# The end of a mixture-of-experts block: the last two experts' results scattered together, the last 2 MB of weights loaded by columns

## The chip, the cores and the metric

One core of a Trainium2 chip runs the kernel. The metric is the device time of one execution in microseconds (us); of several executions the median is given.

## The reference

One residual block on x of 256 tokens x 1024, in float32. The first part is sparse attention and a pooling mixer, merged and added to x. The second part, which takes four fifths of the time, is a mixture of 32 experts of which each token takes 4:

```
logits = tok @ router_w + router_b
topv, topi = top_k(logits, 4);  topw = softmax(topv)
combine = sum(one_hot(topi, 32) * topw[..., None], axis=1)
for e in range(32):
    gu = tok @ w1[e] + b1[e]                       # 1024 -> 2048
    gate = minimum(gu[:, :1024], 7);  lin = clip(gu[:, 1024:], -7, 7)
    act = (lin + 1) * gate * sigmoid(1.702 * gate)
    out = out + combine[:, e:e + 1] * (act @ w2[e] + b2[e])
x = x + out
```

`w1[e]` is 8 MB and `w2[e]` 4 MB.

## The kernel before, in words

Every expert gets 64 slots. For expert e the kernel gathers the rows of its tokens by a matmul with a 0/1 matrix (`pick`, L362), multiplies them with `w1` (`up`, L399), applies the gate on DVE and ACT, transposes the activation, multiplies with `w2` (`down`, L428), and adds the result to the tokens' rows by a matmul with a matrix that holds each slot's token and weight (`scatter`, L437). A loop with five experts in each turn does that with one expert's `up` ahead of the `down` of the one before.

The weights come from HBM in chunks of 2 MB, in pairs where that is possible, into a ring of ten slots; the DMAs stand in one queue, issued by SP, which waits until a slot's reader is done. Every chunk of `w2` holds 4 of the 8 rows that each partition has of it. Of the last chunks SP loads pieces with semaphores of their own: the table `TAIL` (L185) gives the rows of each. `(E - 2, 1)` and `(E - 1, 0)` are halves of 1 MB, and `(E - 1, 1)`, the last 2 MB, comes in parts of 1, 0.5 and 0.5 MB (`load_tail`, L598 to L602).

Everything of 64 slots uses half of the PE array. In `down` an expert's 64 x 1024 result is cut in two halves of 512 columns. The left one goes to partitions 0 to 63 of a bank of PSUM and the right one to partitions 64 to 127 of the same bank, so each matmul has 64 columns of the array and two of them stand one behind the other on its two column halves. One ACT copy brings the bank to SBUF (`out_out`, L846). In `scatter` the 64 slots are the rows of the array, again in pairs: the left result sits on partitions 0 to 63, the right one on 64 to 127, and the placement matrix, transposed, is there twice (`putT`, 128 partitions). For each of the two token tiles (`tt`) and each half it adds to one of four accumulator banks: bank `2 * tt + half`. These four hold the sum over all experts for the whole run.

The order of PE's work is written out by hand. At the end, behind the loop (from the call of `up_last`), it is:

```
down_tail(E - 1, 0, ps_gather, actT_last)
pe.wait_ge(out_ok, E - 1)
scatter(pe, None, range(0, 1))
down_tail(E - 1, 1, ps_gather, actT_last).then_inc(gemm2, 1)
scatter(pe, None, range(1, 2))
pe.wait_ge(out_ok, E)
scatter(pe, acc_done, range(TT), putT_last, out_last)
```

The first two scatters are those of expert 30, whose result ACT copies at L846; the last one is expert 31's, copied at L877, with its placement copied at L871. Then two of the four result tiles are finished by DVE (L1200, with an addition of x) and stored by SP (L635), the other two are copied by ACT (L895), and after both copies ACT issues their stores (L899). SP waits for all four stores.

Of the kernel before, what the change touches and what calls it, by code (L numbers as in the profile page):

```python
# [24 lines left out]
P = 128  # L25
# [15 lines left out]
def block_kernel(nc, x, attn_norm_g, w_in, q_norm_g, k_norm_g, pool_w, pool_b, pool_scale,  # L41
# [44 lines left out]
    with ExitStack() as ctx:  # L86
        def sb(name, shape, dt=F32):
            return ctx.enter_context(nc.sbuf_tensor(name, shape, dt))
# [40 lines left out]
        putT_last, actT_last, out_last = work[:, 5, 0:TT * P], work[:, 6], work[:, 7]  # L129
# [4 lines left out]
        putT = sb("putT", [P, TT * P])  # L134
        bias_pick = sb("bias_pick", [P, SLOTS])
# [39 lines left out]
        ps_gate, ps_lin, ps_out, ps_gather = bank[4:8]  # L175
        first_ps = (ps_gather, bank[3])
# [7 lines left out]
        HALVES, THIRDS = ((0, 2), (2, 4)), ((0, 2), (2, 3), (3, 4))  # L184
        TAIL = {(E - 2, 1): HALVES, (E - 1, 0): HALVES, (E - 1, 1): THIRDS}  # L185
# [3 lines left out]
        def tail_in(e, c, i):  # L189

            return part_in[tail_parts.index((e, c, i))]
# [150 lines left out]
        def w2_wide(e):  # L342

            return expert_w2[0][bass.ds(e, 1), :, :].rearrange("a (p k) n -> p (a k n)", p=P)
# [87 lines left out]
        def scatter(pe, done=None, tiles=range(TT), at=putT, src=out_e):  # L432

            for tt in tiles:
                for half in range(2):
                    rows = halves(half)
                    mm = pe.matmul(acc[2 * tt + half][:, :], at[rows, tt * P:(tt + 1) * P], src[rows, :],  # L437
                                   start=False, stop=True, skip_group_check=True)
                    if done is not None:
                        mm.then_inc(done, 1)  # L440
            return mm
# [30 lines left out]
        def _(sp):  # L472
# [125 lines left out]
            def load_tail(e, c):  # L598

                src = w2_wide(e)[:, c * CHUNK_N:(c + 1) * CHUNK_N]  # L600
                for i, (a, b) in enumerate(TAIL[e, c]):
                    sp.dma_start(chunk_slot(w2_chunk(e, c))[:, a * D:b * D], src[:, a * D:b * D]).then_inc(tail_in(e, c, i), 16)  # L602
# [77 lines left out]
        def _(act):  # L680
# [190 lines left out]
            nc.scalar.copy(putT_last, ps_gather[:, 0:T]).then_inc(put_sb, 1)  # L871
# [3 lines left out]
            out_out(E - 2)  # L875
            act.wait_ge(gemm2, E)
            nc.scalar.copy(out_last, ps_gather[:, :]).then_inc(out_ok, 1)  # L877
# [15 lines left out]
            for tt, j in enumerate((1, 2)):  # L893
                act.wait_ge(acc_done, j + 1)
                nc.scalar.copy(xs[:, tt, (1 - tt) * BANK:(2 - tt) * BANK], acc[j][:, :]).then_inc(s["result_act"], 1)  # L895
            for tt in range(TT):
                cols = slice((1 - tt) * BANK, (2 - tt) * BANK)
                act.wait_ge(s["result_act"], tt + 1)
                act.dma_start(out[0, tt * P:(tt + 1) * P, cols], xs[:, tt, cols]).then_inc(s["stored"], 16)  # L899
# [304 lines left out]
        def _(pe):  # L1204
# [374 lines left out]
            def down_tail(e, c, ps, actT):  # L1579
                for i, (a, b) in enumerate(TAIL[e, c]):  # L1580
                    pe.wait_ge(tail_in(e, c, i), 16)
                    mm = down(pe, chunk_halves(w2_chunk(e, c)), c, range(a, b), ps, actT, True)
                return mm

# [58 lines left out]
            down_tail(E - 1, 0, ps_gather, actT_last)  # L1643
            pe.wait_ge(out_ok, E - 1)
            scatter(pe, None, range(0, 1))
            down_tail(E - 1, 1, ps_gather, actT_last).then_inc(gemm2, 1)
            scatter(pe, None, range(1, 2))
            pe.wait_ge(out_ok, E)
            scatter(pe, acc_done, range(TT), putT_last, out_last)
# [53 lines left out]
```

## Time and profile before

| what | us |
|---|---|
| median of 3 runs | 1113.23 (1112.6 to 1114.18) |
| the profiled execution, its own time | 1112.02 |
| its span, from the first to the last instruction | 1110.3 |
| PE busy | 1075.9 (97%) |
| DMA of the weights, 430.73 MB in the SP queue | 92.1% of 16 engines' span |
| DVE busy, ACT busy | 216.3, 160.8 |

The time of a run holds some 1.7 us that lie outside of the span. PE's busy time is that of overlapping matmuls, which are modelled to their ends, so 97% does not say that PE sets the pace: it waits for the weights in nearly every expert. The chain that ended last names DMA for 33% of the span and PE for 64%.

### The profile page before, as it was taken

The numbers are of one execution on the slowest core, as the hardware profiler recorded it, in microseconds if no ns is written. First come the engines' busy times: TensorE is split into PE (matmuls) and PEld (weight loads), VectorE is DVE, ScalarE is ACT, GpSimd is POOL, SyncE is SP. The second block draws the span as 40 slices with busy tenths as digits, with TensorE's granted clock in tenths as the row PEclk, the third lists the DMA queues.
The fourth block names the chain that finished last, engine by engine and source line by source line (L and its number), as shares of the span: only waits on it lengthen the run. The fifth ranks groups of instructions, "written<-read, shape, count | busy, mean of one in ns | idle before, by whom it ended". The sixth has DMA issues, their size and how long they took to land.

```text
span 1110.3 us, 12071 instructions
## 1 busy us (share of the span) xinstructions
PE 1075.9 (97%) x5114; PEld 458.5 (41%) x5114; DVE 216.3 (19%) x521; ACT 160.8 (14%) x362; POOL 20.5 (2%) x38
## 2 busy tenths in 40 slices
PE   9999999999999999999999999999999999999997
PEld 6478885633333333333333333333233333333332
DVE  2722121321111111211111111111111111111111
ACT  2114201210000111111111111111011111111111
POOL 0006000000000000000000000000000000000000
PEclk9999999999999999999999999999999999999999
DMA  9924627999999999999999999999999999999996
GB/s 338 378 80 150 226 87 319 400 421 429 426 423 424 432 429 433 427 437 430 432 430 431 433 433 433 430 430 430 433 433 433 431 430 430 431 434 432 426 427 276
DMA packets 34891, 432.60 MB, mean 390 GB/s; under 512 B 3612, under 2 KB 5168, under 8 KB 17712
## 3 DMA queue, kind: packets, MB, share of 16 engines
q1 hardware_dynamic: 32672, 430.73, 92.1%
q10 hardware_dynamic: 2192, 1.48, 0.5%
q8 instruction: 21, 0.34, 0.1%
q14 instruction: 6, 0.05, 0.0%
HBM read 431.15 MB, written 1.05 MB: 389 GB/s over the span
## 4 chain that ended last, share of the span: by engine, by line
PE 64%; DMA 33%; DVE 2%; issue 0%; ACT 0%; SPq 0%
DMA ring<-in_expert_w_dram 32%; PE bank L399 24%; PE bank L428 14%; PE bank L1330 5%; PE bank L437 4%; PE bank L1394 2%; PE bank L362 2%; PE bank L1404 2%; PE bank L389 2%; PE bank L1253 2%; PE bank L1314 1%; PE bank L376 1%; PE bank L411 1%; PE bank L381 1%; PE bank L1226 1%; DVE ring L967 1%
## 5 line engine op out<-in xcount | busy, mean ns | idle before, releaser
L399 PE MATMUL bank<-ring,work 128*64 128x512 f32 x2048 | 451.5, 596 | 15.6 <-DMA ring<-in_expert_w_dram 15.6
L399 PEld LDWEIGHTS bank<-ring,work 128*64 128x64 f32 x2048 | 143.3, 137 | 320.8 <-issue 289.6
L428 PE MATMUL bank<-ring,work 128*64 128x512 f32 x992 | 219.4, 593 | 11.4 <-DMA ring<-in_expert_w_dram 11.3
L428 PEld LDWEIGHTS bank<-ring,work 128*64 128x64 f32 x992 | 74.9, 137 | 151.2 <-issue 148.9
L1104 DVE TENSOR_SCALAR work<-bank 128x512 f32<-128x512 f32 x31 | 21.4, 692 | 459.8 <-PE bank L399 459.8
L826 ACT ACTIVATE work<-work 128x512 f32<-128x512 f32 x31 | 19.5, 630 | 497.7 <-DVE work L1104 497.7
L463 DVE TENSOR_TENSOR work<-bank,vecs 128x512 f32<-128x512 f32 x31 | 21.4, 691 | 209.9 <-PE bank L376 209.9
L437 PE MATMUL bank<-work,putT 64*128 64x512 f32 x248 | 61.9, 616 | 0.0
L362 PE MATMUL bank<-xs,pick 128*64 128x512 f32 x248 | 58.5, 592 | 0.0
L1330 PE MATMUL bank<-ring 128*128 128x256 f32 x256 | 56.6, 380 | 0.0
L1330 PEld LDWEIGHTS bank<-ring 128*128 128x128 f32 x256 | 48.2, 190 | 6.7 <-issue 0.3
L846 ACT COPY work<-bank 128x512 f32<-128x512 f32 x31 | 18.2, 587 | 203.4 <-PE bank L428 203.4
L1253 PE MATMUL bank<-ring 128*128 128x512 f32 x96 | 42.3, 595 | 0.0
L418 ACT COPY work<-bank 64x256 f32<-64x256 f32 (+1 forms) x112 | 40.2, 359 | 3.7 <-PE bank L411 2.7
L389 PE MATMUL bank<-b_rows,bias_pick 32*64 32x512 f32 x256 | 34.8, 612 | 0.3 <-ACT work L837 0.3
L362 PEld LDWEIGHTS bank<-xs,pick 128*64 128x64 f32 x248 | 17.7, 137 | 35.0 <-issue 35.0
L437 PEld LDWEIGHTS bank<-work,putT 64*128 64x128 f32 x248 | 21.3, 186 | 19.4 <-issue 15.8
L1404 PE MATMUL bank<-ring,xn 128*128 128x512 f32 (+1 forms) x80 | 28.4, 508 | 0.0
L1114 DVE TENSOR_TENSOR work<-work 128x512 f32<-128x512 f32 x26 | 27.5, 1057 | 0.9
L1253 PEld LDWEIGHTS bank<-ring 128*128 128x128 f32 x96 | 17.9, 190 | 21.0 <-issue 20.9
L454 DVE TENSOR_SCALAR put<-slot_id,place,weight 128x128 f32<-128x128 f32 x64 | 19.3, 343 | 37.6 <-PE bank L381 37.5
L1108 DVE SCALAR_TENSOR_TENSOR work<-work 128x512 f32<-128x512 f32 x31 | 21.4, 692 | 3.2
(210 smaller groups left out, 523.7 us busy)
## 6 DMA issues: line engine op xcount, KB each, us to landing
ring<-in_expert_w_dram SPq DMA_DIRECT2D x70, 4096.0 KB, 39.5
ring<-in_expert_w_dram SPq DMA_DIRECT2D x39, 2048.0 KB, 15.9
ring<-in_expert_w_dram SPq DMA_DIRECT2D x21, 1024.0 KB, 10.5
ring<-in_w_in_dram SPq DMA_DIRECT2D x8, 2048.0 KB, 21.0
ring<-in_w_out_dram SPq DMA_DIRECT2D x2, 2048.0 KB, 8.1
ring<-in_w_branch_attn_dram SPq DMA_DIRECT2D x1, 2048.0 KB, 7.9
ring<-in_w_branch_pool_dram SPq DMA_DIRECT2D x1, 2048.0 KB, 8.9
work<-in_expert_w_dram SPq DMA_DIRECT2D x2, 1024.0 KB, 13.7
```

The lines of the kernel that those rows point to most:

```text
L362: mm = pe.matmul(ps_gather[SLOTS * half:SLOTS * (half + 1), :], pick[:, tt, :], xs[:, tt, half * BANK:(half + 1) * BANK], start=(tt == 0), ...
L389: mm = pe.matmul(dst, bias_pick[rows, :], b1_rows[rows, :], start=first, stop=not first, skip_group_check=True)
L399: mm = pe.matmul(dst, hTe[:, at:at + SLOTS], w[a][:, col:col + BANK], start=(k == 0 and not bias_first), stop=(k == KD - 1 and bias_first) ...
L418: last = nc.scalar.copy(dst[halves(h), :].rearrange("p (j i s) -> p i j s", i=2, s=SLOTS)[:, i, blocks, :], src[halves(i), :].rearrange("p ...
L428: mm = pe.matmul(ps[SLOTS * half:SLOTS * (half + 1), :], actT[:, at:at + SLOTS], w[a // 2][:, col:col + BANK], start=(k == 0), stop=(k == ...
L437: mm = pe.matmul(acc[2 * tt + half][:, :], at[rows, tt * P:(tt + 1) * P], src[rows, :], start=False, stop=True, skip_group_check=True)
L463: return nc.vector.tensor_tensor(hTe.rearrange("p (j h n) -> p j h n", j=4, h=2), ps_gather[:, :].rearrange("p (j h n) -> p j h n", j=4, h ...
L1114: nc.vector.tensor_tensor(by_rows(act_e), lin, sig, ALU.mult).then_inc(glu_ok, 1)
L1253: mm = pe.matmul(dst, hT[:, k, tt * P:(tt + 1) * P], w[:, k, :], start=(k == 0), stop=(k == KD - 1))
L1330: mm = pe.matmul(bank[GATE_BANK[n % 4]][:, b * T:(b + 1) * T], w[:, k, at:at + P], hT[:, k, :], start=(k == 0), stop=(k == KD - 1))
L1394: mm = pe.matmul(bank[2 + 2 * (j % 2) + n][:, b * T:(b + 1) * T], w[:, k, at:at + P], src[:, k, :], start=(k == 0), stop=(k == KA - 1))
L1404: mm = pe.matmul(ps, mergedT[:, k, tt * P:(tt + 1) * P], w[:, k, at:at + cols.stop - cols.start], start=(k == 0), stop=(k == KD - 1))
```

## The change

The last 2 MB of `w2` are cut by columns: first the left 512 columns of all four rows (1 MB), then the right 512 columns of two rows and of the other two (0.5 MB each). For expert 31 the halves of the result go to two banks, the left one to partitions 64 to 127 of bank 7 and the right one to partitions 0 to 63 of bank 5. ACT copies expert 30's left half to partitions 0 to 63 of a tile and expert 31's left half to partitions 64 to 127 of the same tile, and so, the other way round, for the right halves; the placements are put together likewise. One scatter matmul with 128 rows then adds both experts' results to an accumulator bank: first the left half for both token tiles, then the right half. ACT stores each of its tiles right behind its copy. Expert 31's chunk 1 no longer has a scatter ahead of it.

```diff
-        putT_last, actT_last, out_last = work[:, 5, 0:TT * P], work[:, 6], work[:, 7]
+        actT_last = work[:, 6]
+        two_out = (xn[:, 0, 0:BANK], xn[:, 0, BANK:D])
...
+        two_putT = (putT, xn[:, 1, 0:TT * P])
...
+        last_ps = (ps_gather, ps_lin)
...
-        HALVES, THIRDS = ((0, 2), (2, 4)), ((0, 2), (2, 3), (3, 4))
-        TAIL = {(E - 2, 1): HALVES, (E - 1, 0): HALVES, (E - 1, 1): THIRDS}
+        HALVES, COLUMNS = ((0, 2, 0, D), (2, 4, 0, D)), ((0, 4, 0, BANK), (0, 2, BANK, D), (2, 4, BANK, D))
+        TAIL = {(E - 2, 1): HALVES, (E - 1, 0): HALVES, (E - 1, 1): COLUMNS}
...
-                src = w2_wide(e)[:, c * CHUNK_N:(c + 1) * CHUNK_N]
-                for i, (a, b) in enumerate(TAIL[e, c]):
-                    sp.dma_start(chunk_slot(w2_chunk(e, c))[:, a * D:b * D], src[:, a * D:b * D]).then_inc(tail_in(e, c, i), 16)
+                src = w2_wide(e)[:, c * CHUNK_N:(c + 1) * CHUNK_N].rearrange("p (r n) -> p r n", n=D)
+                dst = chunk_slot(w2_chunk(e, c)).rearrange("p (r n) -> p r n", n=D)
+                for i, (a, b, left, right) in enumerate(TAIL[e, c]):
+                    sp.dma_start(dst[:, a:b, left:right], src[:, a:b, left:right]).then_inc(tail_in(e, c, i), 16)
...
             act.wait_ge(put_ps, E)
-            nc.scalar.copy(putT_last, ps_gather[:, 0:T]).then_inc(put_sb, 1)
+            act.wait_ge(put_sb, E - 1)
+            chain.link(nc.scalar.copy(two_putT[1][halves(1), :], putT[halves(1), :]))
+            nc.scalar.copy(two_putT[1][halves(0), :], ps_gather[halves(0), 0:T])
+            nc.scalar.copy(two_putT[0][halves(1), :], ps_gather[halves(1), 0:T]).then_inc(put_sb, 1)
...
-            out_out(E - 2)
-            act.wait_ge(gemm2, E)
-            nc.scalar.copy(out_last, ps_gather[:, :]).then_inc(out_ok, 1)
+            act.wait_ge(gemm2, E - 1)
+            nc.scalar.copy(two_out[0][halves(0), :], ps_out[halves(0), :])
+            nc.scalar.copy(two_out[1][halves(1), :], ps_out[halves(1), :]).then_inc(out_ok, 1)
+            for h in range(2):
+                act.wait_ge(gemm2, E + h)
+                nc.scalar.copy(two_out[h][halves(1 - h), :], last_ps[h][halves(1 - h), :]).then_inc(out_ok, 1)
...
-            for tt, j in enumerate((1, 2)):
-                act.wait_ge(acc_done, j + 1)
-                nc.scalar.copy(xs[:, tt, (1 - tt) * BANK:(2 - tt) * BANK], acc[j][:, :]).then_inc(s["result_act"], 1)
-            for tt in range(TT):
+            for n, tt in enumerate((1, 0)):
                 cols = slice((1 - tt) * BANK, (2 - tt) * BANK)
-                act.wait_ge(s["result_act"], tt + 1)
+                act.wait_ge(acc_done, n + 2)
+                nc.scalar.copy(xs[:, tt, cols], acc[1 + tt][:, :]).then_inc(s["result_act"], 1)
+                act.wait_ge(s["result_act"], n + 1)
                 act.dma_start(out[0, tt * P:(tt + 1) * P, cols], xs[:, tt, cols]).then_inc(s["stored"], 16)
...
+            def down_last(c, i):
+
+                a, b, left, right = TAIL[E - 1, c][i]
+                w = chunk_halves(w2_chunk(E - 1, c))
+                pe.wait_ge(tail_in(E - 1, c, i), 16)
+                for r in range(a, b):
+                    k = c * W2_ROWS + r
+                    for half in range(left // BANK, right // BANK):
+                        col = r % 2 * D + half * BANK
+                        mm = pe.matmul(last_ps[half][halves(1 - half), :], actT_last[:, k * SLOTS:(k + 1) * SLOTS],
+                                       w[r // 2][:, col:col + BANK], start=(k == 0), stop=(k == KD - 1))
+                return mm
+
+            def scatter_two(half):
+
+                for tt in range(TT):
+                    pe.matmul(acc[2 * tt + half][:, :], two_putT[half][:, tt * P:(tt + 1) * P], two_out[half],
+                              start=False, stop=True, skip_group_check=True).then_inc(acc_done, 1)
...
-            down_tail(E - 1, 0, ps_gather, actT_last)
-            pe.wait_ge(out_ok, E - 1)
-            scatter(pe, None, range(0, 1))
-            down_tail(E - 1, 1, ps_gather, actT_last).then_inc(gemm2, 1)
-            scatter(pe, None, range(1, 2))
-            pe.wait_ge(out_ok, E)
-            scatter(pe, acc_done, range(TT), putT_last, out_last)
+            for i in range(2):
+                down_last(0, i)
+            down_last(1, 0).then_inc(gemm2, 1)
+            down_last(1, 1)
+            down_last(1, 2).then_inc(gemm2, 1)
+            for half in range(2):
+                pe.wait_ge(out_ok, E + half)
+                scatter_two(half)
```

PE's order from the last expert's chunk 1 on. Before (of its eight scatter matmuls the last two, on banks 2 and 3, follow behind the rows; `part_in4` to `part_in6` are the three parts of the last 2 MB, banks 0 to 3 the accumulators):

```order
L437 MATMUL bank0<-work,putT 128x512 [waits out_ok]
L437 MATMUL bank1<-work,putT 128x512
L428 MATMUL bank7<-ring,work 64x512 [waits part_in4]
L428 MATMUL bank7<-ring,work 64x512 x3
L428 MATMUL bank7<-ring,work 64x512 [waits part_in5]
L428 MATMUL bank7<-ring,work 64x512
L428 MATMUL bank7<-ring,work 64x512 [waits part_in6]
L428 MATMUL bank7<-ring,work 64x512
L437 MATMUL bank2<-work,putT 128x512
L437 MATMUL bank3<-work,putT 128x512
L437 MATMUL bank0<-work 128x512 [waits out_ok]
L437 MATMUL bank1<-work 128x512
```

The same place with the change:

```order
L1603 MATMUL bank7<-ring,work 64x512 [waits part_in4]
L1603 MATMUL bank7<-ring,work 64x512 x3
L1603 MATMUL bank5<-ring,work 64x512 [waits part_in5]
L1603 MATMUL bank5<-ring,work 64x512
L1603 MATMUL bank5<-ring,work 64x512 [waits part_in6]
L1603 MATMUL bank5<-ring,work 64x512
L1610 MATMUL bank0<-xn,putT 128x512 [waits out_ok]
L1610 MATMUL bank2<-xn,putT 128x512
L1610 MATMUL bank1<-xn 128x512 [waits out_ok]
L1610 MATMUL bank3<-xn 128x512
```

Four scatter matmuls have gone, among them the two that stood ahead of the first part; the four left matmuls of the chunk now stand together ahead of the four right ones.

ACT's order from expert 31's gate to the last copy of a result, before:

```order
L869 ACTIVATE work<-work 128x64x4 [waits gate_ok] x2
L871 COPY work<-bank 128x256 [waits put_ps]
L418 COPY work<-bank 64x2x64 [waits actT_ps]
L418 COPY work<-bank 64x2x64 x3
L418 COPY work<-bank 64x2x64 [waits actT_ps]
L418 COPY work<-bank 64x2x64 x3
L846 COPY work<-bank 128x512 [waits glu_ok,gemm2]
L877 COPY work<-bank 128x512 [waits gemm2]
```

And with the change:

```order
L873 ACTIVATE work<-work 128x64x4 [waits gate_ok] x2
L876 COPY xn<-putT 64x256 [waits put_sb,put_ps]
L877 COPY xn<-bank7 64x256 [waits act_step]
L878 COPY putT<-bank7 64x256
L421 COPY work<-bank4 64x2x64 [waits actT_ps]
L421 COPY work<-bank4 64x2x64 x3
L421 COPY work<-bank5 64x2x64 [waits actT_ps]
L421 COPY work<-bank5 64x2x64 x3
L883 COPY xn<-bank6 64x512 [waits gemm2]
L884 COPY xn<-bank6 64x512
L887 COPY xn<-bank7 64x512 [waits gemm2]
L887 COPY xn<-bank5 64x512 [waits gemm2]
```

One copy of the placement has become three, and two copies of results four, each of 64 partitions.

## Rows read from the trace of the kernel before

**Rows 1.** Chain that ended last, in order of time from 1055 us: start, us, what
```profile
core 0 of [0], span 1110.3 us
...
1055.85 39.88 DMA ring<-in_expert_w_dram
...
1098.76 3.58 PE bank L428 x16
1102.35 2.83 PE bank L437 x12
...
1105.19 0.69 DVE xs L1200
```
**Rows 2.** Timeline of PE, 1095 to 1105 us: start, us, engine, line, operation, shapes, records
```profile
1095.76 0.20 PEld L428 LDWEIGHTS bank<-ring,work 128*64 128x64 f32 x4 [1.19 <-DMA ring<-in_expert_w_dram]
1095.77 1.94 PE L428 MATMUL bank<-ring,work 128*64 128x512 f32 x8 [0.30 <-DMA ring<-in_expert_w_dram]
1097.63 1.13 PE L437 MATMUL bank<-work,putT 64*128 64x512 f32 x4
1098.69 3.65 PE L428 MATMUL bank<-ring,work 128*64 128x512 f32 x16
...
1101.75 0.60 PE L428 MATMUL bank<-ring,work 128*64 128x512 f32 x2
1102.28 1.13 PE L437 MATMUL bank<-work,putT 64*128 64x512 f32 x4
1103.24 1.88 PE L437 MATMUL bank<-work 64*128 64x512 f32 x8
```
**Rows 3.** Timeline of PE, 11 to 26 us: matmuls that are not in pairs
```profile
11.17 1.89 PE L1231 MATMUL bank<-ring 128*68 128x256 f32 x8
...
18.53 7.03 PE L1253 MATMUL bank<-ring 128*128 128x512 f32 x16
```
**Rows 4.** Stretches: 2 KB rows alone, then the experts' loads; last columns PEclk, DMA share, GB/s
```profile
40.00:45.00 5.00, 5.00 (x13) 2.24 (x12) 4.42 (x17) 0.60 (x1) 0.00 (x0) 1.00 1.05 387
1060.00:1070.00 10.00, 10.00 (x50) 3.79 (x46) 2.47 (x4) 2.67 (x7) 0.00 (x0) 1.00 1.00 428
```
**Rows 5.** Timeline of ACT, 1086 to 1103 us
```profile
1086.97 0.36 ACT L871 COPY work<-bank 128x256 f32<-128x256 f32 x1
1089.98 2.18 ACT L418 COPY work<-bank 64x128 f32<-64x128 f32 x8 [2.65 <-PE bank L411]
1093.79 0.59 ACT L846 COPY work<-bank 128x512 f32<-128x512 f32 x1 [1.64 <-PE bank L428]
1102.39 0.59 ACT L877 COPY work<-bank 128x512 f32<-128x512 f32 x1 [8.02 <-PE bank L428]
```
**Rows 6.** Stores by SP (L635), by ACT (L899); DMA from 1104 to 1111 us in 40 slices
```profile
1105.01 0.35 SPq L635 DMA_DIRECT2D out_dram<-xs  x1
1105.91 1.20 SPq L635 DMA_DIRECT2D out_dram<-xs  x1
DMA to landing us min/median/max: 2.5/3.3/4.0
DMA to landing us min/median/max: 3.6/3.6/3.7
GB/s 0 0 0 0 0 0 0 0 94 0 117 351 374 398 363 351 374 363 176 23 117 386 398 398 398 386 374 386 199 23 23 12 0 0 0 0 0 0 0 0
```
**Rows 7.** PE after long waits (timeline), and stretches around them with PEclk
```profile
672.55 0.65 PE L399 MATMUL bank<-ring,work 128*64 128x512 f32 x2 [0.86 <-DMA ring<-in_expert_w_dram]
789.18 8.78 PE L399 MATMUL bank<-ring,work 128*64 128x512 f32 x32 [2.16 <-DMA ring<-in_expert_w_dram]
934.95 2.37 PE L399 MATMUL bank<-ring,work 128*64 128x512 f32 x10 [2.15 <-DMA ring<-in_expert_w_dram]
...
790.00:792.00 2.00, 2.00 (x8) 0.51 (x6) 0.00 (x0) 0.00 (x0) 0.00 (x0) 0.50 0.91 393
792.00:794.00 2.00, 2.00 (x10) 0.66 (x8) 0.00 (x0) 0.00 (x0) 0.00 (x0) 0.67 1.03 442
934.00:936.00 2.00, 1.05 (x6) 0.48 (x8) 0.00 (x0) 0.00 (x0) 0.00 (x0) 1.00 1.06 459
```

More of the change, by code:

```diff
@@ L430, in down, with scatter @@
             return mm
-        def scatter(pe, done=None, tiles=range(TT), at=putT, src=out_e):
-            for tt in tiles:
+        def scatter(pe, done=None):
+            for tt in range(TT):
                 for half in range(2):
                     rows = halves(half)
-                    mm = pe.matmul(acc[2 * tt + half][:, :], at[rows, tt * P:(tt + 1) * P], src[rows, :],
+                    mm = pe.matmul(acc[2 * tt + half][:, :], putT[rows, tt * P:(tt + 1) * P], out_e[rows, :],
                                    start=False, stop=True, skip_group_check=True)
@@ L1579, in down_tail @@
             def down_tail(e, c, ps, actT):
-                for i, (a, b) in enumerate(TAIL[e, c]):
+                for i, (a, b, left, right) in enumerate(TAIL[e, c]):
                     pe.wait_ge(tail_in(e, c, i), 16)
@@ L1583, in down_tail @@
                 return mm
+            def down_last(c, i):
[10 more added lines that the diff above has]
+            def scatter_two(half):
+                for tt in range(TT):
+                    pe.matmul(acc[2 * tt + half][:, :], two_putT[half][:, tt * P:(tt + 1) * P], two_out[half],
+                              start=False, stop=True, skip_group_check=True).then_inc(acc_done, 1)
             def gather_expert(e):
```

## The prediction

> **What bounds the kernel now.** I read the chain of waits first. For the last 55 us it has one DMA entry, which ends at 1095.73 (1055.85 + 39.88), and after it nothing but PE, one DVE addition and what follows it [rows 1]. So up to 1095.7 the stream of weights sets the time. The change leaves that stretch as it is, and everything is decided in the 14.6 us behind it. The timeline of PE shows them: the second half of expert 31's chunk 0 (8 records, from 1095.77), the first two scatter matmuls of expert 30 (4 records, 1097.63), chunk 1 (16 records, 1098.69), the other two of expert 30 (1102.28), and expert 31's four (8 records, 1103.24) [rows 2]. Each fp32 matmul of the program leaves two records. Then come an addition of 0.69 us, from 1105.19 [rows 1], the last store, issued at 1105.91 and landed 4.0 us later, at 1109.9 [rows 6], and 0.4 us to the end of the span.
>
> The unit of PE's time: 16 records of two column halves take 3.65 us [rows 2]. Two start together every 0.429 us (7 x 0.429 + 0.64 = 3.64), so a pair of program matmuls on the two halves costs 0.858 us, and the halves run side by side. Records that have the array to themselves are no cheaper: 16 of 512 elements take 7.03 us (15 x 0.429 + 0.59), and eight with only 68 active columns and 256 elements take 1.89 us, 0.216 each [rows 3].
>
> **The change, part by part.** All sums run against the profiled execution: span 1110.3, its own time 1112.02, which is 1.2 below the median of the three runs, 1113.23.
>
> (a) The last 2 MB come in rows of 2 KB (512 columns) instead of 8 and 4 KB. In the stretch where this kernel loads 2 KB rows alone the DMA moves 387 GB/s; near the end it moves 428 [rows 4]. Left half: 1.049 MB / 387 = 2.71 us, landing at 1095.73 + 2.71 = 1098.44; now the same bytes need 2.45, 1098.18. The two right quarters follow at 1099.79 and 1101.15. The bounds of this term are 0 (428) and +0.26 us on the left half. I take +0.26, since the rows of that size are the nearest. The three parts were handed over long before they move, so their issue hides behind the 40 us of queue [rows 1].
>
> (b) Expert 30's first two scatter matmuls leave the gap in which PE waits for chunk 1. They cost nothing there but about 0.25 us (PE starts chunk 1 at 1098.69, though the bytes are due at 1098.18). After the change PE starts the left half at 1098.44 + 0.04 = 1098.48, 0.2 earlier than now, and idles about 0.9 us before it.
>
> (c) Chunk 1 loses its pairs. Its left half is four matmuls on one column half of the array (bank 7), its right half four on the other (bank 5). By rows 3 four unpaired matmuls take 4 x 0.858 = 3.43 us, as long as all eight take now. Left ones start at 1098.48, 1099.34, 1100.20 and 1101.05. The first right matmul stands directly behind the last left one, on the other half. Such neighbours start together now: four weight loads within 0.20 us, and 8 records in 1.94 us = 3 x 0.429 + 0.65 [rows 2], with the second half's first pass not held up by the first half's second pass. So I let them overlap by one matmul: the right four run from 1101.05 to 1104.48, both quarters landed before they are due (1101.05 and 1102.77). Now the same work ends at 1101.75 + 0.43 = 1102.18. The term is **+2.3 us**. From below: the halves run freely from their landings, 1099.8 at the earliest (-1.2 us). From above: no overlap (+0.86).
>
> (d) The scatter now comes whole behind it. Before: 6 program matmuls in three pairs, from 1102.28. After: 4 with all 128 rows, which fill the array and can't pair. Their first record starts 0.52 us after the last one of the right half, as at the switch of 1101.75 to 1102.28 [rows 2]: 1104.05 + 0.52 = 1104.57. Eight records by 0.429: the last starts at 1104.57 + 3.00 = 1107.57, against 1104.53 now (1103.24 + 1.88 - 0.59). With (c) that makes **+3.0 us** on PE; the scatter's own share is 0.75.
>
> (e) ACT. The left copy is released 0.64 us after the last left record starts (1101.48; as 1101.75 to 1102.39 now [rows 2, 5]), takes 0.59 and is done at 1102.7, well before 1104.57. The right one: 1104.05 + 0.64 + 0.59 = 1105.28, needed by the third scatter matmul at 1106.29, so it is hidden with 1.0 us left; without that cover the 0.5 us wait of today's copy would come back. Copying 64 partitions instead of 128 I count at the full 0.59. Expert 30's copy becomes two, 1.18 us from 1093.8, and nobody asks for them before 1104. The placement's copy (0.36 at 1086.97) becomes three and a wait, 1.2 us, into an idle stretch that lasts until 1089.98 [rows 5]. All zero.
>
> (f) The stores. Results now leave PE 0.86 us apart instead of two and two, so the last addition starts at 1107.57 + 0.66 = 1108.23, ends at 1108.92 and its store is issued at 1108.95. Today the last of four stores, all issued within 0.9 us, lands after 4.0 us, and the first of its queue after 2.5 [rows 6]. The first bytes move 0.85 us after the first issue, and 256 KB at some 370 GB/s take 0.7 [rows 6]. Bounds for the new last store: 1.9 us (0.85, 0.7 and the 0.35 that the end of the span shows behind the last landing) and 4.0. I take 2.2, between 1.9 and the 2.5 of the store that had its engines nearly alone: **-1.8 us**. The Trainium skill ("DMA: Bandwidth & Descriptors", section on latency) gives a DMA a fixed cost of about 2 us, most of it the receipt from memory; with 0.6 for the bytes that would be 2.6, and the sum 0.4 higher. No row shows a store alone.
>
> Sum: 1108.95 + 2.2 + 0.4 = 1111.5, against 1110.3: +3.0 - 1.8 = **+1.2 us**. On the median: 1113.2 + 1.2 = **1114.4 us**. That is 0.1%, inside the 0.2% (2.2 us) that a measurement of this kernel can tell from no change.
>
> **The rivals.**
>
> A, the forecast: one matmul of overlap between the halves, short last store; 0.44, 1114.4.
>
> B, no such overlap: the right half's first pass waits for the last left matmul's second pass, at 1101.48, or for its end, 1101.91. The 1.94 us for 8 records [rows 2] speak against it, since strict order of passes would give 1.72 + 0.59 = 2.31. Price +0.43 to +0.86, 1114.8 to 1115.3; 0.15. The Trainium skill ("TensorE: Matmul & The Clock Gate", Part 3, the mechanism of packing small matmuls) has this rule: matmuls start and end strictly in program order.
>
> C, the halves run apart. PE looks further ahead, and the right half starts with its landings: 1099.83, 1100.69, 1101.55, 1102.41, end 1103.26. The scatter's last record starts at 1106.35 and all ends 1.2 earlier: 1113.2. For it: pairs already pass each other by a pass. Against: nothing shows a longer lead. 0.18.
>
> D, a lone column half streams at twice the rate. The left half would end at 1100.2, the right one with its last quarter at 1102.1, the scatter's last record start at 1105.4: 2.2 less, 1112.2. The 68-column rows [rows 3] speak against it. 0.05; only together with a very short store is this faster by over 0.2%.
>
> E, the slower side: the store saves nothing. Behind each pair of stores the DMA moves 23 GB/s for a while, one engine's worth [rows 6]; if that engine is late for another reason than four stores at once, the last store takes 4.0 us as now, and the whole delay of PE shows: +3.0, 1116.2. It decides from a landing of 3.2 us upward (+2.2). For it: the ACT queue's first store took 3.6 us, with hardly more beside it than its fellow's 2.5 [rows 6]. 0.13.
>
> F, the clock. The removed scatter makes PE idle for about 0.9 us. After an idle of 2.16 us the granted clock was 0.50 from 790 to 792, 1.2 GHz instead of 2.4, and 0.67 over the next 2 us, which costs 2 x 0.50 + 2 x 0.33 = 1.7 us; an equal idle at 932 to 935 and one of 0.86 at 672 changed nothing [rows 7]. Price +1.7: 1116.1. 0.05.
>
> **How the numbers follow.** A to D lie between 1112.2 and 1115.3, E and F at 1116. The range 1112.4 to 1116.0 takes in A, B and C with their bounds and some of E. Faster by over 0.2% (under 1111.0) needs D and more: 0.05. Slower by over 0.2% (over 1115.4) is E, F and the upper edge of B with a store of 2.6: 0.20. The rest, 0.75, is no change.
>
> **What would show each step.** (a) PE's first record of the left half near 1098.5, DMA near 390 GB/s in the last 5 us. (b) An idle of about 0.9 us on PE before it, named DMA, clock at 1.0. (c) The lone left records 0.429 us apart, the first right record with the seventh left one; all 16 in 6.0 us (6.9 in B, 4.8 in C). (d) Eight scatter records in 3.6 us with no gap between the third and the fourth, and 0.52 us before the first. (e) No wait on ACT's copy in front of the third scatter matmul. (f) Four stores issued about 0.9 us apart, the last landing 2.2 us after its issue; 2.6 or 4.0 would name the page's figure or E. The forecast is wrong if lone halves run at another pace than 0.429 us a record, or if the last store does not gain at least 1 us.

## The result, and the profile after

Over 21 runs each the change takes 1114.42 us (median; 1112.85 to 1115.92) and the kernel before 1113.21 us (1111.47 to 1114.46). The ratio is 1.0014 with an interval of 1.0008 to 1.002: a little slower, inside of the 0.2% that the prediction called no change. The medians lie 1.2 us apart. The profiled executions have spans of 1111.3 and 1110.3 us, so of that they show 1.0.

The chain that ended last, in order of time from 1060 us (start, us, what), answers to [rows 1]:

```profile
1059.97 38.35 DMA ring<-in_expert_w_dram
1098.32 0.04 issue
1098.37 5.42 PE bank L1603 x16
1103.79 3.65 PE bank L1610 x8
1107.43 0.02 issue
1107.45 0.69 DVE xs L1209
```

The weights' stream still ends the wait at which the tail begins, but one part later, at 1098.32. Behind it stand 5.42 us of chunk 1 where 3.65 stood, then the scatter, the addition and the store. The timeline of PE and of its weight loads (PEld) over the same stretch, with the idle time ahead in brackets, answers to [rows 2]:

```profile
1095.65 1.94 PE L1603 MATMUL bank<-ring,work 128*64 128x512 f32 x8 [0.35 <-DMA ring<-in_expert_w_dram]
1098.37 5.42 PE L1603 MATMUL bank<-ring,work 128*64 128x512 f32 x16 [0.77 <-DMA ring<-in_expert_w_dram]
...
1099.28 0.14 PEld L1603 LDWEIGHTS bank<-ring,work 128*64 128x64 f32 x1 [0.29 <-issue]
1099.70 0.14 PEld L1603 LDWEIGHTS bank<-ring,work 128*64 128x64 f32 x1 [0.29 <-issue]
1100.13 0.19 PEld L1603 LDWEIGHTS bank<-ring,work 128*64 128x64 f32 x3 [0.29 <-issue]
1100.56 0.19 PEld L1603 LDWEIGHTS bank<-ring,work 128*64 128x64 f32 x2 [0.24 <-issue]
...
1103.72 1.98 PE L1610 MATMUL bank<-xn,putT 128*128 128x512 f32 x4
...
1105.11 0.19 PEld L1610 LDWEIGHTS bank<-xn 128*128 128x128 f32 x1 [0.24 <-issue]
1105.54 1.88 PE L1610 MATMUL bank<-xn 128*128 128x512 f32 x4
```

Up to 1099.70 one weight load stands every 0.43 us: the left matmuls alone. At 1100.13 there are three within 0.19 us. Two of them are the right half's, which joins beside the fifth left record. Between the two groups of scatter records nothing is lost: the eight start from 1103.72 to 1106.83 (1105.54 + 1.88 - 0.59). ACT's timeline, to be held against [rows 5]:

```profile
1086.93 0.40 ACT L876 COPY xn<-putT 64x256 f32<-64x256 f32 x1
1087.37 0.37 ACT L877 COPY xn<-bank 64x256 f32<-64x256 f32 x1
1087.74 0.37 ACT L878 COPY putT<-bank 64x256 f32<-64x256 f32 x1
1089.82 2.17 ACT L421 COPY work<-bank 64x128 f32<-64x128 f32 x8 [1.71 <-PE bank L414]
1093.63 0.58 ACT L883 COPY xn<-bank 64x512 f32<-64x512 f32 x1 [1.64 <-PE bank L431]
...
1102.05 0.58 ACT L887 COPY xn<-bank 64x512 f32<-64x512 f32 x1 [7.25 <-PE bank L1603]
1103.82 0.58 ACT L887 COPY xn<-bank 64x512 f32<-64x512 f32 x1 [1.19 <-PE bank L1603]
```

The last copy ends at 1104.40. The third scatter matmul starts at 1105.54 and its weight load, which waits for that copy, at 1105.11, so 0.7 us are left. A copy of 64 partitions takes 0.58, as long as one of 128 took. Three views answer to [rows 6]. The last store in SP's timeline:

```profile
1108.17 0.35 SPq L639 DMA_DIRECT2D out_dram<-xs  x1
```

The landings of the two stores of SP and of the two of ACT, by their lines:

```profile
DMA to landing us min/median/max: 2.6/2.7/2.8
DMA to landing us min/median/max: 2.8/3.0/3.2
```

The DMA from 1104 to 1111.3 in 40 slices:

```profile
GB/s 0 0 0 0 0 0 0 0 0 0 0 0 0 281 370 348 337 180 337 370 370 213 11 22 112 348 382 393 382 404 382 393 135 22 22 22 0 0 0 0
```

The last store takes 2.8 us from its issue to its landing where it took 4.0. In the stretch of the last 2 MB's left half the DMA moves 384 GB/s at a granted clock of 1.00 (last three columns: PEclk, DMA share, GB/s):

```profile
1095.70:1098.30 2.60, 1.89 (x8) 0.44 (x8) 0.00 (x0) 0.00 (x0) 0.00 (x0) 1.00 1.04 384
```

### The profile page after: what moved, and what is told of

Same layout as the page of the kernel before. It is cut to its first block, busy times and chain, and to the rows that moved or that the text cites. A ratio compares the mean times of both kernels' runs of the same rounds, so it can differ in the third digit from the quotient of the medians.

```text
span 1111.3 us, 12059 instructions
## 1 busy us (share of the span) xinstructions
PE 1077.7 (97%) x5106; PEld 459.4 (41%) x5106; DVE 216.3 (19%) x521; ACT 162.8 (15%) x366; POOL 20.6 (2%) x38
## 4 chain that ended last, share of the span: by engine, by line
PE 64%; DMA 32%; DVE 2%; SPq 0%; issue 0%; ACT 0%; POOL 0%; POOLq 0%
DMA ring<-in_expert_w_dram 32%; PE bank L402 24%; PE bank L431 13%; PE bank L1339 5%; PE bank L440 3%; PE bank L1403 2%; PE bank L365 2%; PE bank L1413 2%; PE bank L392 2%; PE bank L1262 2%; PE bank L1323 1%; PE bank L379 1%; PE bank L414 1%; PE bank L384 1%; PE bank L1235 1%; DVE ring L976 1%
## 5 line engine op out<-in xcount | busy, mean ns | idle before, releaser
L402 PE MATMUL bank<-ring,work 128*64 128x512 f32 x2048 | 451.5, 596 | 15.4 <-DMA ring<-in_expert_w_dram 15.4
L431 PE MATMUL bank<-ring,work 128*64 128x512 f32 x960 | 212.1, 593 | 11.1 <-DMA ring<-in_expert_w_dram 11.0
L440 PE MATMUL bank<-work,putT 64*128 64x512 f32 x240 | 59.6, 615 | 0.0
## 6 DMA issues: line engine op xcount, KB each, us to landing
work<-in_expert_w_dram SPq DMA_DIRECT2D x2, 1024.0 KB, 13.9
```

Source lines behind the costliest of these rows:

```text
L402: mm = pe.matmul(dst, hTe[:, at:at + SLOTS], w[a][:, col:col + BANK], start=(k == 0 and not bias_first), stop=(k == KD - 1 and bias_first) ...
L431: mm = pe.matmul(ps[SLOTS * half:SLOTS * (half + 1), :], actT[:, at:at + SLOTS], w[a // 2][:, col:col + BANK], start=(k == 0), stop=(k == ...
L440: mm = pe.matmul(acc[2 * tt + half][:, :], putT[rows, tt * P:(tt + 1) * P], out_e[rows, :], start=False, stop=True, skip_group_check=True)
```

## The experiments

Two theories stood at the start. **The lone halves** (matmuls for one column half of the array with none for the other beside them): the change loses time because chunk 1's matmuls no longer run in pairs, and the rest costs nothing on balance. **The column cut is sound**, and the cost comes from elsewhere (the scatter of 128 rows, smaller DMA rows, the order of the stores). A second question was open for the stores: what the last one waits for.

From one profiled execution to the next the whole end shifts by up to 2.2 us, since the stream of weights ends earlier or later (this start lies between 1095.47 and 1097.68). Traces are therefore compared by **the tail**: the span less the start of the second part of expert 31's chunk 0 on PE. It is 1110.3 - 1095.77 = 14.5 us before and 1111.3 - 1095.65 = 15.7 with the change. Every tail is that of one trace. x3_right_first (1118.0 us), x4_two_stores (1114.65), x6_lone_pieces (1116.23), x7_store_behind (1113.78), x10_no_second_pass (1112.87) and x11_before_no_second_pass (1111.78) ran once each, so for them only the trace speaks.

### By rows again, in pairs (x1_rows)

```diff
-        HALVES, COLUMNS = ((0, 2, 0, D), (2, 4, 0, D)), ((0, 4, 0, BANK), (0, 2, BANK, D), (2, 4, BANK, D))
+        HALVES, THIRDS = ((0, 2, 0, D), (2, 4, 0, D)), ((0, 2, 0, D), (2, 3, 0, D), (3, 4, 0, D))
...
-            down_last(1, 0).then_inc(gemm2, 1)
-            down_last(1, 1)
-            down_last(1, 2).then_inc(gemm2, 1)
+            for i in range(3):
+                mm = down_last(1, i)
+            mm.then_inc(gemm2, 2)
```

> Undoes the column cut alone: the last 2 MB by rows (1, 0.5, 0.5 MB) and in pairs, the two experts' scatter and the order of the stores stay. If the lone column halves are what the change pays with, the 16 records of chunk 1 take 3.65 us instead of 5.42, from about 1098.2; the left copy ends at about 1102.5, the first of 8 scatter records starts at 1102.6 (1103.72 with the change), the last at 1105.6 (1106.82), and the span is 1.1 to 1.2 us shorter than the change's 1111.3, about 1110.1. If instead the cut is what makes this end work (left copy and scatter early), taking it away exposes both ACT copies and the span is 1111.3 or more.

Ratio to the kernel before 0.9999 (0.999 to 1.0008), 1113.07 us. Timeline of PE:

```profile
1097.57 1.94 PE L1603 MATMUL bank<-ring,work 128*64 128x512 f32 x8 [0.30 <-DMA ring<-in_expert_w_dram]
1100.03 3.65 PE L1603 MATMUL bank<-ring,work 128*64 128x512 f32 x16 [0.53 <-DMA ring<-in_expert_w_dram]
1104.36 1.98 PE L1610 MATMUL bank<-xn,putT 128*128 128x512 f32 x4 [0.68 <-ACT xn L887]
```

The tail is 14.6 us (1112.2 - 1097.57), 1.0 less than the change's. The span alone, 1112.2, would speak for the other case of the expectation; but this execution (1113.98 us) was the slowest of eleven with a median of 1113.07, and its tail began 1.9 us later than that of the change's trace. Chunk 1 is back at 3.65 us. Against that, the left copy now stands open: PE idles 0.68 us for it. Both things were expected, and the first is the larger. The merged scatter and the new order of the stores together neither cost nor gain anything against the kernel before that these runs could tell.

### The column cut alone (x2_lone_halves)

The kernel before, with `load_tail` and `TAIL` of the change and a `down` that takes the sides:

```diff
-        def down(pe, w, c, rows=range(W2_ROWS), ps=ps_out, actT=actT_e, wide=False):
+        def down(pe, w, c, rows=range(W2_ROWS), ps=ps_out, actT=actT_e, wide=False, sides=range(2)):
...
-                for half in range(2):
+                for half in sides:
...
```

> The kernel before with the column cut alone: same parts as the change, chunk 1 as four left and then four right matmuls, but expert 30's and expert 31's scatters apart and placed as before, all stores as before. If lone halves cost 0.43 us a record with the right half starting beside the third left matmul, chunk 1's records span 5.4 us instead of 3.65, the last scatter record starts 1.8 to 1.9 us later (1106.4) and the span is 1112.1, ratio 1.0016. If the cut costs only the 0.2 us of its smaller DMA rows, the span is 1110.5.

Ratio 1.0014 (1.0005 to 1.0023), 1114.59 us. Timeline of PE:

```profile
1095.47 1.94 PE L428 MATMUL bank<-ring,work 128*64 128x512 f32 x8 [0.31 <-DMA ring<-in_expert_w_dram]
1097.34 1.13 PE L437 MATMUL bank<-work,putT 64*128 64x512 f32 x4
1098.40 5.42 PE L428 MATMUL bank<-ring,work 128*64 128x512 f32 x16
```

5.42 us again, and a tail of 16.3 (1111.8 - 1095.47), 1.8 over the kernel before. So the cut by columns alone costs 1.8 us in the trace, and undoing it alone gives 1.0 back. The difference is near the 0.68 us for which x1_rows waits for the left copy: in the change that copy lies under the right half's matmuls. Chunk 1 starts 2.93 us behind the start of the tail here and 2.92 before, so behind the two scatters, which keep PE busy past the landing, the smaller DMA rows cost nothing. That answers the first question: the loss comes from the lone halves.

### How far PE looks ahead (x3_right_first, x6_lone_pieces)

In the change the right half joined earlier than forecast. Either it only waited for its data, or PE lets it pass a fixed lead. First the right quarters are loaded ahead of the left half:

```diff
-                for i, (a, b, left, right) in enumerate(TAIL[e, c]):
+                order = (1, 2, 0) if (e, c) == (E - 1, 1) else range(len(TAIL[e, c]))
+                for i in order:
+                    a, b, left, right = TAIL[e, c][i]
```

> The change with the right quarters loaded ahead of the left half, PE's order unchanged: when the first left matmul starts (about 1101.0) all of the right half lies in SBUF. If PE looks a fixed way ahead, the first right record again starts with the fifth left one, 1.75 us behind the first, and the 16 records span 5.42 us. If in the changed kernel the right half only waited for its data, it starts within 0.1 us of the first left record and the 16 span 3.65 us. If the halves overlap by one matmul, as forecast, it starts with the seventh, 2.6 us behind.

The timeline of the weight loads:

```profile
1101.51 0.29 PEld L1605 LDWEIGHTS bank<-ring,work 128*64 128x64 f32 x2 [4.16 <-DMA ring<-in_expert_w_dram]
1102.42 0.23 PEld L1605 LDWEIGHTS bank<-ring,work 128*64 128x64 f32 x1 [0.62 <-issue]
1103.28 0.23 PEld L1605 LDWEIGHTS bank<-ring,work 128*64 128x64 f32 x1 [0.62 <-issue]
1104.13 0.23 PEld L1605 LDWEIGHTS bank<-ring,work 128*64 128x64 f32 x1 [0.62 <-issue]
1104.70 0.19 PEld L1605 LDWEIGHTS bank<-ring,work 128*64 128x64 f32 x3 [0.34 <-issue]
```

The stretches around them (the column ahead of the last two is PEclk):

```profile
1101.50:1103.50 2.00, 1.99 (x3) 0.74 (x4) 0.00 (x0) 0.00 (x0) 0.00 (x0) 0.50 0.00 0
1105.50:1108.00 2.50, 2.50 (x10) 0.74 (x6) 0.00 (x0) 0.58 (x1) 0.00 (x0) 1.00 0.00 0
```

The right half's data had been there since before 1101.5, and still it joins with the fifth left record, as in the change. So it is a limit on how far PE runs ahead, and not the data. The time in microseconds came out differently from what was expected (6.84 us for the 16 records), because PE had idled 3.28 us and the clock was granted at 0.50, 1.2 GHz: a left record takes 0.86 us there. The tail is 20.0 us, 4.3 over the change's: 2.5 from the longer wait for the left half, 1.4 from the clock (6.84 against 5.42), 0.4 at the last store.

Then pieces of 256 columns, all on the column half that the change uses:

```diff
-                        col = r % 2 * D + half * BANK
-                        mm = pe.matmul(last_ps[half][halves(1 - half), :], actT_last[:, k * SLOTS:(k + 1) * SLOTS],
-                                       w[r // 2][:, col:col + BANK], start=(k == 0), stop=(k == KD - 1))
+                        for q in range(2):
+                            at, col = q * QUARTER, r % 2 * D + half * BANK + q * QUARTER
+                            mm = pe.matmul(last_ps[half][halves(1 - half), at:at + QUARTER], actT_last[:, k * SLOTS:(k + 1) * SLOTS],
+                                           w[r // 2][:, col:col + QUARTER], start=(k == 0 and q == 0), stop=(k == KD - 1),
+                                           skip_group_check=True)
```

> The same pieces of 256 columns, but both on the column half that the change uses, so chunk 1 is eight unpaired left matmuls and eight unpaired right ones of 0.43 us each. It tells what PE counts in looking ahead: if it is instructions (two matmuls with their weight loads), the first right record starts with the 13th left one, 2.6 us behind the first, and the records of chunk 1 span about 6.3 us; if it is time (1.75 us behind the first, as in the change), with the 9th, and they span 5.4 us.

```profile
1100.08 6.31 PE L1605 MATMUL bank<-ring,work 128*64 128x256 f32 x32 [0.63 <-DMA ring<-in_expert_w_dram]
```

Every record is half as long and the 32 take 6.31 us, as the count by matmuls gives it: 16 left records at 0.216, of which the last four run beside the right half. The weight loads agree: behind the first two they stand singly, 0.215 us apart, up to 1102.51, and at 1102.73, 2.65 us behind the first, there are three within 0.19 us. Lead by time would have given 5.4. In three kernels the right half joins as the last but one of the left matmuls starts (each is two records), whether such a matmul takes 0.86 us or 0.43, and also in x3_right_first, where at half the clock 3.2 us had passed since the first.

### Pieces of 256 columns, in pairs (x5_quarters, x5_again)

The same pieces go to both column halves, so that each of the left and the right half is done in pairs:

```diff
...
+                        for q in range(2):
+                            col = r % 2 * D + half * BANK + q * QUARTER
+                            mm = pe.matmul(last_ps[half][halves(q), 0:QUARTER], actT_last[:, k * SLOTS:(k + 1) * SLOTS],
+                                           w[r // 2][:, col:col + QUARTER], start=(k == 0), stop=(k == KD - 1))
...
-                nc.scalar.copy(two_out[h][halves(1 - h), :], last_ps[h][halves(1 - h), :]).then_inc(out_ok, 1)
+                for q in range(2):
+                    last = nc.scalar.copy(two_out[h][halves(1 - h), q * QUARTER:(q + 1) * QUARTER], last_ps[h][halves(q), 0:QUARTER])
+                last.then_inc(out_ok, 1)
```

> The change with every 512-column half of expert 31's down matmuls cut in two pieces of 256 columns that go to the two column halves of the array, so that the left half and the right half of chunk 1 are each done in pairs; two more ACT copies. If unpaired halves are what the change pays with, chunk 1's 32 records end 1.4 us earlier against its first one than in the change, the scatter starts at 1102.0 instead of 1103.7, its last record at about 1105.1 instead of 1106.8, and the time is 1.5 to 1.7 us under the change: ratio to the kernel before 0.9995, 1112.7. If pieces of 256 columns cost more than half of 512 (weight loads of 0.14 us for matmuls of 0.22), or the two extra copies show, little is left of that and the ratio stays at 1.001.

```profile
1097.12 1.95 PE L1607 MATMUL bank<-ring,work 128*64 128x256 f32 x16 [0.43 <-DMA ring<-in_expert_w_dram]
1099.75 3.67 PE L1607 MATMUL bank<-ring,work 128*64 128x256 f32 x32 [0.68 <-DMA ring<-in_expert_w_dram]
1103.35 1.98 PE L1614 MATMUL bank<-xn,putT 128*128 128x512 f32 x4
1105.17 1.88 PE L1614 MATMUL bank<-xn 128*128 128x512 f32 x4
```

3.67 us and no wait for the copy: the tail is 14.0 us (1111.1 - 1097.12), 1.7 under the change and 0.5 under the kernel before, to 0.1 us as expected. The ratio is 1.0001 (0.9992 to 1.001). A second time:

> The version in pieces of 256 columns a second time, unchanged, beside the one with five parts: its trace was 0.55 us shorter than that of the kernel before between the second part of chunk 0 and the end, while its ratio was 1.0001 with an interval of 0.9992 to 1.001. If the trace tells the truth the ratio of this run lies at 0.9995; if something outside of the tail costs it 0.5 us, it stays at 1.000.

Ratio 1.0 (0.9991 to 1.0009), tail 13.9. The 0.5 us by which both traces are under the kernel before would be 0.9995, which both intervals hold; the timed runs can neither show nor refute it. Against the change the intervals meet only at their edges (1.0008 to 1.002 against 0.9992 to 1.001 and 0.9991 to 1.0009), and the tail is 1.7 to 1.8 us shorter in both traces.

### Five parts (x9_five_parts)

```diff
-        HALVES, COLUMNS = ((0, 2, 0, D), (2, 4, 0, D)), ((0, 4, 0, BANK), (0, 2, BANK, D), (2, 4, BANK, D))
+        HALVES, COLUMNS = ((0, 2, 0, D), (2, 4, 0, D)), ((0, 2, 0, BANK), (2, 4, 0, BANK), (0, 2, BANK, D), (2, 3, BANK, D), (3, 4, BANK, D))
...
-            down_last(1, 0).then_inc(gemm2, 1)
-            down_last(1, 1)
-            down_last(1, 2).then_inc(gemm2, 1)
+            for i in range(5):
+                mm = down_last(1, i)
+                if i in (1, 4):
+                    mm.then_inc(gemm2, 1)
...
```

> The version in pieces of 256 columns, with the last 2 MB in five parts instead of three: left half in 0.5 and 0.5 MB, right half in 0.5, 0.25 and 0.25 MB (two semaphores of the start of the kernel are used a second time). PE then need not wait for the whole left half, and only one row's matmuls (0.43 us) follow the last landing. If PE's late start on the left half is what delays its end, the last record of chunk 1 starts 5.4 us behind the first of the second part of chunk 0 instead of 5.9, and the span less that start is 13.5 us instead of 14.0; ratio to the kernel before 0.9991. If two more transfers slow the last 2 MB by as much, it stays at 14.0.

Ratio 1.0001 (0.9992 to 1.001), tail 14.5 (1110.4 - 1095.92): a miss. PE gained 0.3 us of the 0.5 expected: the scatter starts 5.9 us behind the second part of chunk 0 (1101.82) and not 6.2. But the last store, issued 0.3 us earlier against that start, took 3.8 us to land and not 2.9. That pointed to the stores.

### What the last store waits for (x4_two_stores, x7_store_behind)

Without ACT's two stores:

```diff
-            sp.wait_ge(s["stored"], 16 * 2 * TT)
+            sp.wait_ge(s["stored"], 16 * TT)
...
-                act.wait_ge(s["result_act"], n + 1)
-                act.dma_start(out[0, tt * P:(tt + 1) * P, cols], xs[:, tt, cols]).then_inc(s["stored"], 16)
```

> The change without ACT's two stores (half of the output is not written; the copies stay), so SP's last store has the DMA to itself. If the 2.8 us of the last store come from a backlog of one DMA engine behind the stores ahead of it, it lands after 2.2 to 2.3 us and the span is 0.5 us shorter than 1111.3. If a store of this kind simply takes 2.8, it still does, and the span stays within 0.1 of 1111.3.

```profile
DMA to landing us min/median/max: 2.4/3.4/4.4
```

The last store lands after 2.4 us, 0.4 less than in the change, and the tail is 0.4 shorter (15.2 us). But the first store, with no other beside it, takes 4.4. No backlog of stores explains that.

The kernel before, with each of ACT's stores behind its copy:

```diff
             for tt, j in enumerate((1, 2)):
+                cols = slice((1 - tt) * BANK, (2 - tt) * BANK)
                 act.wait_ge(acc_done, j + 1)
-                nc.scalar.copy(xs[:, tt, (1 - tt) * BANK:(2 - tt) * BANK], acc[j][:, :]).then_inc(s["result_act"], 1)
-            for tt in range(TT):
-                cols = slice((1 - tt) * BANK, (2 - tt) * BANK)
+                nc.scalar.copy(xs[:, tt, cols], acc[j][:, :]).then_inc(s["result_act"], 1)
                 act.wait_ge(s["result_act"], tt + 1)
```

> The kernel before with ACT's two stores each issued directly behind its copy. If the spacing of the four results on PE is what shortened the last store (4.0 to 2.8 us), this edit changes little: the first ACT store is issued 0.2 us earlier, the last SP store still lands 3.8 to 4.0 us after its issue, and the span less the start of expert 31's second down part stays at 14.5 us. If the order of ACT's copies and stores was the cause, the last landing takes about 3 us and that difference falls by 1 us.

Tail 14.5 (1112.1 - 1097.61). SP's stores land after 3.4 and 3.7 us, and the last to land is now ACT's second, after 3.9: the order of ACT's work is not the cause.

### The fetch beside the stores (x10_no_second_pass, x11_before_no_second_pass)

In the section on queues every trace up to here has a 16 KB packet of the kind "instruction" in the stretch of the stores (x3_right_first has two), a fetch of code. It is there in [rows 6] too: the slice of 94 GB/s, 0.175 us long, holds 16 KB. In x4_two_stores, with half of the stores, it took 1.8% of 16 engines over 7 us, 2.0 us of one engine; in x9_five_parts, with its late last store, 1.9. The programs of PE, ACT, DVE and SP jump there over the code of a second pass. Both kernels without it (of four such blocks the start of ACT's is shown):

```diff
-            with act.If(most_reg > FIRST_SLOTS):
-                with act.Fori(0, PASSES * E) as n:
...
```

> The change without the code of the second pass (the blocks that run only if an expert has over 64 tokens, which none has here). In every trace so far one 16 KB fetch of instructions stands beside the first stores and takes 1.0 to 2.0 us of one DMA engine; that engine completes the first store's part 1.4 to 2.3 us after the other fifteen. If the jump over the second pass's code brings that fetch, it is gone or earlier, and the last store lands 2.0 to 2.3 us after its issue instead of 2.8. If the slow engine is slow for another reason, the landing still takes 2.8.

> The kernel before without the code of the second pass. If the fetch is the reason that four stores close together wait on each other, the last store lands about 3.0 us after its issue (0.9 to the first bytes, 1.4 for the pair, the rest its end) instead of 4.0. If it is the four stores themselves, 3.8 to 4.0 stays.

The landings of all four stores of x10_no_second_pass, then of SP's two in x11_before_no_second_pass:

```profile
DMA to landing us min/median/max: 2.0/2.1/2.1
```

```profile
DMA to landing us min/median/max: 2.1/2.6/3.2
```

2.0 to 2.1 us (2.05 from here on) instead of 2.8 for the last store of the change, 3.2 instead of 4.0 for that of the kernel before, and no 16 KB packet in the stretch any more. It has not moved: another one stands between 1099 and 1100 in the traces of both kernels, with the second pass and without, and the whole run has 20 of them on that queue instead of 21. The tails fall to 14.9 and 13.8 us. So about 0.75 us of either kernel's end is that fetch. What the 3.2 has over 2.05 is four stores at once: the DMA moves 340 to 420 GB/s without a gap from 1106.4 to 1109.2. In x10_no_second_pass the four stores follow one another after 0.8 to 1.0 us, with about 0.7 us of bytes each, and all land after 2.0 to 2.1, so at that spacing they do not hold each other up; the 0.4 us of x4_two_stores was no price of the stores alone. The change's gain at the last store is the same with the fetch (1.2 us, 4.0 to 2.8) and without it (1.15, 3.2 to 2.05), so it does not hang on the fetch.

### Both (x12_both)

> The version with pieces of 256 columns and five parts, and without the code of the second pass. Its two gains should add: the last store issued 10.4 us behind the start of the second part of chunk 0 and landed 2.05 us later, so the span less that start is 12.8 us, against 14.5 in the kernel before and 15.7 in the change. Ratio to the kernel before 0.9985. If the earlier fetch collides with the weights instead and costs as much there, the ratio stays at 0.9995 or above.

Ratio 0.9983 (0.9974 to 0.9992), 1111.11 us, tail 12.7 (1109.8 - 1097.14): faster than the kernel before beyond its interval, which also ends below that of the change (1.0008 to 1.002). Of the 1.9 us of tail against the kernel before, 0.7 is what x11_before_no_second_pass gets as well by leaving out the second pass; the other 1.1 comes with the pieces, the five parts and the rest of the change. The end of its PE timeline and the landings of its four stores:

```profile
1101.07 1.95 PE L1566 MATMUL bank<-ring,work 128*64 128x256 f32 x16 [0.21 <-DMA ring<-in_expert_w_dram]
1102.95 1.98 PE L1573 MATMUL bank<-xn,putT 128*128 128x512 f32 x4
```

```profile
DMA to landing us min/median/max: 2.0/2.0/2.1
```

It is not a full replacement: an input with an expert of over 64 tokens needs the second pass.

## Why the prediction was right, and where it was not

The time was forecast at 1114.4 us and measured at 1114.42. That is better than the working deserves, and luck in part: two of its terms were off by 0.9 and 0.6 us, and they mostly cancelled.

| step | forecast | measured |
|---|---|---|
| (a) left half landed | 1098.44, 387 GB/s | 1098.32, 384 GB/s |
| (b) idle of PE before it | 0.9, clock 1.0 | 0.77, clock 1.00 |
| (c) first right record | 1101.05 | 1100.14 |
| (c) last record of chunk 1 starts | 1104.05 | 1103.20 |
| (d) scatter's first and last record | 1104.57, 1107.57 | 1103.72, 1106.83 |
| (e) wait for the right copy, spare to the matmul | none, 1.0 | none, 1.1 |
| (f) last store issued, then to its landing | 1108.95, 2.2 | 1108.17, 2.8 |
| end of the span | 1111.5 | 1111.3 |

(a) as said: the rate of 2 KB rows alone, from the kernel's own start, held to 1%. Against rows of 4 and 8 KB the half came 0.26 us later in this trace (2.72 us behind the start of the tail, 2.46 in x1_rows); in x10_no_second_pass, x4_two_stores, x5_quarters and x6_lone_pieces it was 2.59 to 2.65, so 0.13 to 0.19.

(b) as said for the idle. But the price of the two scatters ahead of chunk 1 is not "about 0.25 us": the prediction's own 1098.69 - 1098.18 is 0.51, and the measured one 0.46 (2.92 before, 2.46 in x1_rows). No sum used the 0.25; the earlier start of 0.2 us was right.

(c) had the right mechanism and the wrong size. Lone halves do run at 0.429 us a record, which x2_lone_halves shows by itself. But "I let them overlap by one matmul" should have been two. The pairs of [rows 2] only show that a neighbour passes one waiting pass; they cannot show more, because in pairs there is nothing more to pass. The value was taken at the lower bound of what the row supports. With the measured lead the term is +1.4 us (1101.75 to 1103.20) instead of +2.3. Rival C had the direction, but not the cause: its halves started with their landings, at 1099.8, and PE was not that free. Rival B fell, and so did D, since the left records stand 0.43 us apart. So did, for these matmuls, the rule of the Trainium skill ("TensorE: Matmul & The Clock Gate", Part 3, the mechanism) that matmuls start strictly in program order: in the change's trace a matmul for the other column half starts while three passes ahead of it in the program have not yet started.

(d) as said, but for 0.1 us that the first record took longer than 0.429.

(e) as said, but the copy is awaited by the weight load, 0.43 us ahead of its matmul, so that 0.7 us were to spare and not 1.1.

(f) had the wrong price. The row of 4.0 us was read as four stores at once, and the 2.5 of the first as a store nearly alone. Both also held a share of one slow DMA engine, busy with a fetch of instructions (without it they take 3.2 and 2.1): the last store of the change takes 2.05 us without the fetch (forecast 2.2) and 2.8 with it. The term had the spacing of the stores right and put the fetch at nothing. Rival E named that engine as something that might be late for another reason, and gave it 0.13. It was late, by less than the 3.2 us from which it would have decided. The estimate from the Trainium skill ("DMA: Bandwidth & Descriptors", section on latency), its fixed cost of about 2 us plus 0.6 for the bytes, 2.6 in all, is over the 2.05 of x10_no_second_pass.

Rival F did not occur; x3_right_first, with an idle of 3.28 us, shows what it would have looked like.

So the change loses 2.3 us on PE and gets 1.2 back at the stores. Counted from the start of the tail PE loses 2.4: 1.8 in chunk 1 and 0.85 in the scatter (3.1 us from its first to its last record, where six matmuls in pairs took 2.25), less 0.2 by which chunk 1 starts earlier.

## What to carry to other kernels

Cutting the last transfer so that one half can be finished early is worth little if each half then uses half of the array: cut the output so that every early piece still fills all column groups (x5_quarters), which costs two small copies. Here that took back the loss; a gain over the kernel before the timed runs did not show until five parts and the removed second pass came on top (x12_both). When two terms of opposite sign make a small sum, check each against its own row, since the total can be right for the wrong reasons. At the very end of a program look for what else the DMA does there, instruction fetches included.

## What the runs showed of the hardware

- The first matmul for one column half of the array joined as the last but one of the fp32 matmuls ahead of it for the other half started, and no earlier: with the fifth of eight left records in the change and in x3_right_first, with the thirteenth of sixteen in x6_lone_pieces.
- fp32 matmuls of 512 columns that all go to one column half of the array took the 0.43 us a record that pairs on both halves take: 5.42 us for chunk 1 instead of 3.65; in pieces of 256 columns on both halves it was 3.67.
- A 16 KB instruction packet stood beside the first stores, for 1.0 us of one DMA engine in the kernel before and 2.0 us in x4_two_stores; without it the last 256 KB store of the change landed in 2.05 us instead of 2.8.
- An ACT copy of 512 elements took 0.58 us on 64 partitions, 0.59 on 128; one of 256 elements from PSUM 0.37 and 0.36.
- The granted clock fell to 0.50 after an idle of 3.28 us and stayed at 1.00 after one of 0.77.
